# A macaron transformer kernel: x's first slice ahead of the first weights, and the norm's turn two slices later

## What is computed

```python
def rms_norm(x, g):
    y = xf * lax.rsqrt(jnp.mean(xf * xf, axis=-1, keepdims=True) + EPS)
    return (y * g).astype(x.dtype)

def swiglu(x, w_gate, w_up, w_down):        # 1024 -> 2816 -> 1024
    return (jax.nn.silu(x @ w_gate) * (x @ w_up)) @ w_down

for i in range(2):
    x = x + 0.5 * swiglu(rms_norm(x, ffn1_norm[i]), ...)
    x = x + (even_mixer, odd_mixer)[i](rms_norm(x, mix_norm[i]), ...)
    x = x + 0.5 * swiglu(rms_norm(x, ffn2_norm[i]), ...)
```

## Time and profile before

| what | value |
|---|---|
| median of three runs | 1895.54 us (1895.01 to 1895.95) |
| the profiled execution's time | 1896.99 us |
| its span, first to last instruction | 1895.2 us |
| TensorE busy | 1865.2 us, 98% |
| DVE busy | 1458.9 us, 77% |
| ACT busy | 1022.7 us, 54% |
| POOL busy | 193.8 us, 10% |

### The profile page before, as it was taken

One profiled execution on the slowest core, in us unless ns is written; L12 is line 12 of the kernel. 1 busy time (PEld: TensorE's weight loads), 2 busy tenths in 40 slices (PEclk: granted clock), 3 DMA queues, 4 the chain that ended last, 5 costly groups with the idle time before them and its releaser, 6 DMA issues.

```text
span 1895.2 us, 31481 instructions
## 1 busy us (share of the span) xinstructions
PE 1865.2 (98%) x11916; PEld 1661.6 (88%) x11916; DVE 1458.9 (77%) x2346; ACT 1022.7 (54%) x1656; POOL 193.8 (10%) x251
## 2 busy tenths in 40 slices
PE   7999999999999999999999999999999999999999
PEld 6899899888779899998889989887778789899997
DVE  8879587577679788597877859657988879697684
ACT  7546264477776355364645526455456766364451
POOL 1311010000001011010011101011111001011010
PEclk9999999999999999999999999999999999999999
DMA  7666662221136565463465556176765376575441
GB/s 235 162 201 184 177 165 66 100 67 68 57 111 178 173 167 152 149 174 109 134 175 156 151 150 173 45 174 159 166 152 132 79 203 170 163 185 158 133 117 67
DMA packets 94790, 271.67 MB, mean 143 GB/s; under 512 B 10504, under 2 KB 10760, under 8 KB 94640
## 3 DMA queue, kind: packets, MB, share of 16 engines
q1 hardware_dynamic: 63456, 201.22, 31.0%
q0 software_dynamic: 29232, 64.50, 19.9%
q10 hardware_dynamic: 1952, 3.93, 1.1%
HBM read 223.07 MB, written 2.77 MB: 119 GB/s over the span
## 4 chain that ended last, share of the span: by engine, by line
PE 88%; DVE 7%; ACT 3%; issue 2%; DMA 0%; ACTq 0%; DVEq 0%
PE ps_unit L817 13%; PE ps_unit L818 13%; PE ps_unit L819 13%; PE ps_y L880 6%; PE ps_y L882 6%; PE ps_y L881 6%; PE ps_s L880 4%; PE ps_s L882 4%; PE ps_s L881 4%; PE ps_t L880 4%; PE ps_t L882 4%; PE ps_t L881 4%; PE ps_s L817 1%; PE ps_s L818 1%; PE ps_s L819 1%
## 5 line engine op out<-in xcount | busy, mean ns | idle before, releaser
L1429 ACT ACTIVATE gw_hi<-gu 128x512 fp32r<-128x512 f32 (+1 forms) x400 | 318.9, 799 | 153.5 <-PE ps_s L882 69.0
L1961 DVE TENSOR_TENSOR gw_lo<-gu,gw_hi 128x512 fp32r<-128x512 f32 (+1 forms) x400 | 354.4, 901 | 40.5 <-ACT gw_hi L1429 33.5
L817 PE MATMUL ps_unit<-a_hi,w_hi 128*128 128x512 f32 x892 | 351.7, 394 | 5.5 <-DVE w_lo L1891 2.8
L818 PE MATMUL ps_unit<-a_lo,w_hi 128*128 128x512 f32 x892 | 348.3, 390 | 0.0
L819 PE MATMUL ps_unit<-a_hi,w_lo 128*128 128x512 f32 x845 | 329.4, 390 | 0.0
L1363 ACT ACTIVATE w_hi<-raw 128x1024 fp32r<-128x1024 f32 (+1 forms) x125 | 125.3, 1003 | 304.6 <-PE ps_unit L819 300.7
L817 PEld LDWEIGHTS ps_unit<-a_hi,w_hi 128*128 128x128 f32 x892 | 167.8, 188 | 45.2 <-DVE w_lo L1891 5.1
L2098 DVE TENSOR_TENSOR t<-ps_unit,half 128x512 f32<-128x512 f32 x96 | 66.4, 691 | 171.8 <-PE ps_unit L819 171.4
L818 PEld LDWEIGHTS ps_unit<-a_lo,w_hi 128*128 128x128 f32 x892 | 167.9, 188 | 33.0
L819 PEld LDWEIGHTS ps_unit<-a_hi,w_lo 128*128 128x128 f32 x845 | 158.9, 188 | 33.7
L1891 DVE TENSOR_TENSOR w_lo<-raw,w_hi 128x1024 fp32r<-128x1024 f32 (+1 forms) x125 | 143.8, 1151 | 13.0 <-ACT w_hi L1363 12.9
(11 more groups left out here) (332 smaller groups left out, 4875.4 us busy)
## 6 DMA issues: line engine op xcount, KB each, us to landing
gu<-gu_stream_dram SPq DMA_DIRECT2D x176, 512.0 KB, 5.2
raw<-w_stream_dram SPq DMA_DIRECT2D x136, 512.0 KB, 3.3
gu<-gu_stream_dram SPq DMA_DIRECT2D x80, 256.0 KB, 3.0
gu<-gu_stream_dram POOLq DMA_DIRECT2D x80, 256.0 KB, 4.1
gu<-gu POOLq DMA_DIRECT2D x80, 256.0 KB, 3.3
w_lo<-raw POOLq DMA_DIRECT2D x28, 512.0 KB, 5.3
raw<-w_stream_dram SPq DMA_DIRECT2D x32, 384.0 KB, 3.9
w_lo_3rd<-raw POOLq DMA_DIRECT2D x15, 512.0 KB, 5.1
```

The lines of the kernel that those rows point to most:

```text
L817: pe.matmul(ps, lhs_hi, rhs_hi, start=first, stop=False)
L818: pe.matmul(ps, lhs_hi, rhs_lo, start=False, stop=False)
L1429: act.activation(gw_hi[:, w, :], src, ACT.Copy).then_inc(gw_hi_done, 1)
L1961: dve.tensor_tensor(gw_lo[:, w, :], src, gw_hi[:, w, :].bitcast(F32), ALU.subtract).then_inc(gw_lo_done, 1)
```

## The change

Two edits. In the second plain tile `spread_norm` moves from behind slice 4 (the third in order) to behind slice 1 (the fifth). This holds in all four feed-forward phases. At the start of the kernel, slice 0 of x is loaded first on SP instead of on ACT's queue, its high and low parts are made before the first weights' parts, and its square and the copy into `acc` come after both parts of the first weights instead of between them.

```diff
+            x_load(0)
             gu_load(0)
             for d in range(1, KT):
                 x_load(d)
...
                     if k == 0:
                         square_sum(i)
-                    if k == 4:
+                    if k == 1:
                         spread_norm(i)
...
             def split_x(i, d):
-
+                high_x(i, d)
+                square_x(i, d, d)
+
+            def high_x(i, d):
                 negative = PHASES[i] == "ffn" and d % 2
                 scale = minus(i * KT + d) if negative else gain("norm", i * KT + d)
                 act.activation(xs_hi[:, d, :], xt_tile(d), ACT.Copy, scale=scale).then_inc(x_hi_done, 1)
-                square_x(i, d, d)
...
             act.dma_start(vec[:, :], vec_in).then_inc(vec_landed, 16)
-            act.dma_start(xt_tile(0), xt_in[0]).then_inc(x_landed[0], 16)
...
             act.wait_ge(vec_landed, 16)
+            act.wait_ge(x_landed[0], 16)
+            high_x(0, 0)
             act.wait_ge(s1_loaded[0], 16)
             for part in range(2):
                 act.activation(gw_hi[:, part, :], gu[:, part, :], ACT.Copy).then_inc(gw_hi_done, 1)
-                if part == 0:
-                    act.wait_ge(x_landed[0], 16)
-                    split_x(0, 0)
+            square_x(0, 0, 0)
             plain_high(0, 1)
...
             def split_x(i, d):
+                low_x(i, d)
+                square_added(i, d)
...
             dve.wait_ge(vec_landed, 16)
+            low_x(0, 0)
             for part in range(2):
                 dve.wait_ge(gw_hi_done, part + 1)
                 dve.tensor_tensor(gw_lo[:, part, :], gu[:, part, :], gw_hi[:, part, :].bitcast(F32), ALU.subtract).then_inc(gw_lo_done, 1)
-                if part == 0:
-                    split_x(0, 0)
+            square_added(0, 0)
             plain_low(0, 1)
```

More of the change, by code:

```diff
@@ L1893, in split_x, with low_x @@
             def split_x(i, d):
+                low_x(i, d)
+                square_added(i, d)
+            def low_x(i, d):
                 negative = PHASES[i] == "ffn" and d % 2
@@ L1898, in split_x @@
                                          ALU.mult, ALU.subtract).then_inc(x_lo_done, 1)
-                square_added(i, d)
             def square_added(i, p):
```

## The result

The changed kernel takes 1900.38 us in the median of nine runs, against 1895.59 us for the kernel before: ratio 1.0025, 95% interval 1.0016 to 1.0033. It is slower by 4.8 us, and the forecast was 1900.3. The profiled execution took 1903.53 us, the longest of the nine, so its rows are compared with rows and not with the medians.

A forecast was written before the change was run, and what follows sets the result against it. PE, busy 98% of the span, was taken as the bound; − 1.4 us at the start plus 4 × 1.56 for the transposes gave + 4.8, so 1895.54 + 4.8 = 1900.3 us, range 1897.0 to 1902.6.

The forecast's parts named there:

- What bounds: Whole kernel: PE is busy 98% of the span, so an edit counts only by what it changes in PE's idle time.
- The gain at the start: Kernel start: second weights' high part at 7.11 us instead of 8.53, so PE's unbroken work starts 1.42 us sooner.
- `vec`'s release at 4.93: Kernel start: ACT's wait for `vec` ends at 4.93 us as before and decides when slice 0's high part begins.
- hidden by 0.2 us: Kernel start: second weights land by 6.9 us, before ACT needs them at 7.11, so their landing costs nothing.
- The clock rise: PE at the start: rise follows 5.9 us of unbroken work, keeping 1.4 us; other cases keep 0.7 or 2.9.
- The landings: DMA at the start: the skill's fit gives 3.2 us for 512 KB, trace 3.9 and 5.3; by it some 2 us gain.
- The move of the transposes: Second plain tile, four ffn phases: DVE copies 2.54 us later, slack 1.14, bubble 0.11; PE pays 1.56 us per phase.
- Slack larger than read: Rival, chain behind DVE's copy: delay is absorbed, only the start's gain counts, 1894.1 us; chance 0.08.
- Given back later: Rival, down projection's first group ends: PE's 0.6 us waits absorb the delay, 2.4 us in all, 1897.9; chance 0.12.
- PE pays the whole: Rival, ffn phases: a step without slack makes PE pay DVE's whole delay, + 10.6 us, 1904.7; chance 0.10.
- The start gains nothing: Rival, kernel start: second weights land 1.4 us later than worked out, `plain_high` waits, 1901.8 us; chance 0.04.
- The first phase: First ffn phase: DVE, arriving at 30.2 us, waits for the transposes until 32.0; same price, 1.56 us.

The follow-up runs named there:

- e1_start_only: Changed kernel with the transposes back behind slice 4, so only the start edit against the kernel before: 1894.17 us against 1895.88, ratio 0.9991.
- e7_squares_later: Start edit alone, with slice 0's square and copy into `acc` moved still later, against the kernel before: 1894.93 us, ratio 0.9995.
- e10_load_only: Kernel before with only slice 0 of x loaded first on SP, ACT's and DVE's order unchanged: 1894.87 us against 1895.81, ratio 0.9995.
- e2_turn_only: Kernel before with only the transposes moved behind slice 1, start unchanged: 1901.63 us against 1895.88, ratio 1.003.
- e6_filled: Changed kernel with work not needing `rstd` moved ahead of the wait on DVE and ACT, against the kernel before: 1894.88 us against 1895.85, ratio 0.9993.
- e3_turn_after_6: Changed kernel with the transposes behind slice 6, the fourth in order, against the kernel before: 1894.6 us, ratio 0.9992.
- e4_turn_after_3: Changed kernel with the transposes behind slice 3, the sixth in order, against the kernel before: 1907.57 us, ratio 1.0057.
- e8_turn_after_5: Changed kernel with the transposes behind slice 5, the seventh in order, against the kernel before: 1915.2 us against 1895.81, ratio 1.0103.

## Why the prediction was right

- **What bounds.** PE's chain with one order of other engines beside it: right. The moved transposes cost at PE what exceeded the slack, to 0.1 us in each of the four phases.
- **The gain at the start**, 1.4 us: measured − 1.7 alone, 1.31 at PE's second start. The size was right, the steps to it were not all, and that it came out is partly luck. I kept `vec`'s release at 4.93 from the kernel before; with the new load it landed by 4.1 in every profile. So the first weights decide, and not `vec`. They released ACT at 5.65 in the kernel after, at the 5.6 that I had named as the point past which I would be wrong, and the two errors nearly cancelled (7.22 against 7.11 for the second weights). In the other profiles they landed where I had them, by 5.2. There PE's second start was 1.7 to 1.9 us sooner where the second weights came in time, and 0.9 to 1.0 where they did not (e1_start_only, e7_squares_later, e10_load_only): that these are hidden by 0.2 us did not hold there.
- **The clock rise.** It came after some 5 us of work instead of 5.9, and PE gains half of that difference, 0.5 us; inside the bounds given. So PE was 1.8 us ahead behind the rise, and not 1.4. No row stood behind the 2.9 us by which the rise might come sooner; the earliest here, 3.0 us after the second start in e7_squares_later, is just that. The Trainium skill (TensorE: Matmul & The Clock Gate, Part 1) says that the default state is throttled and that activity releases it. The profiles agree, but loosely: the two with the old start rose at 16.4 and 17.5 us, the ten with the new one or its load between 13.4 and 15.9, and from the start of unbroken work it took between 3.0 and 6.2. So up to 1.6 us, half of that spread, is chance in any one execution, and the forecast's 1.4 can be right for the median only.
- **The landings.** The fit of the Trainium skill (DMA: Bandwidth & Descriptors, Anatomy of one DMA) gives, as an estimate, 2.6 us for 256 KB; slice 0 landed in 3.1. So the trace is slower than the fit here too. The section states the fit for transfers that the gpsimd path issues, and these are issued on SP's queue, so it was a rough guide to begin with, which the prediction did not say. By the fit the gain would have been some 2 us; 1.7 was measured alone, too near to tell the two apart.
- **The move of the transposes**, 1.56 us a phase, 6.2 in all: 1.47 to 1.57 in each phase of the trace, 6.1 in all, and + 5.75 in the times of e2_turn_only; the 0.45 between is under what the times can tell. PE's wait came in two pieces, for the low weights and for the second of the four `ps_s` steps. The sum had left the first out as falling inside the second, and that held in the total. That a wait in the queue and not the position costs is shown by e6_filled, the slack of 1.1 us by e3_turn_after_6 (DVE 1.04 us late, at most 0.2 us at PE).
- **The rivals.** "Slack larger than read" is excluded by e2_turn_only, + 3.4 us at least, and by e3_turn_after_6 and e4_turn_after_3 on both sides of the edge. "Given back later" is excluded: the waits at the ends of groups stay as they were, five, 2.8 us in all, before and after. "PE pays the whole" is excluded by the 0.5 and 0.4 us waits and the 1.57 us that they cost. "The start gains nothing" is excluded by PE's second start, 0.9 to 1.9 us sooner in every profile with the new load.
- **The first phase** cost nearly as the others, 1.47 us: two PE waits of 0.53 and 0.45 us. DVE waited 1.3 us, under the 1.8 expected; 0.3 of that is what PE had gained beyond the 1.4.

No version is faster than the kernel before beyond doubt. The fastest, e1_start_only, is 1.7 us under it with an interval that touches 1.0.

## What to carry to other kernels

Moving a step to where its own engine does not wait is not free when another engine takes the result in order: price the delay along the consumer's queue, subtract the slack at the row where the bounding engine first needs its end, and pay only the rest. If the step must be late, put work ahead of the wait that does not need it. Read the slack from the tightest consumer, and check every phase that shares the code, not the one for which the edit was made.

## What was not expected

A wait of 1.9 us on TensorE can halve the granted clock for some 3 us, at 0.9 us of cost between the same matmuls of one kernel (0.7 each in the times: 1.4 us over the queue's price, two of four phases). It did so in four of eight such waits in two profiles of the same kernel, in different phases. Waits of 3.3 us did it in four of four, at 0.9 us each in the times. In the second mixer the clock fell in all twelve profiles: in eleven behind or during a wait of 1.3 us, and in e8_turn_after_5, at 1495.9 us, with no wait over 0.2 us in the 20 us ahead. So a short wait alone does not say whether the clock will fall; what else has to come together no run here separates.

At the start the granted-clock column does not show the half rate. Stretches of the kernel after (the same columns as above, granted clock third from the end):

```profile
11.00:15.00 4.00, 4.00 (x11) 3.12 (x10) 4.00 (x7) 3.98 (x8) 0.00 (x0) 1.00 1.03 384
16.00:20.00 4.00, 4.00 (x19) 3.23 (x18) 4.00 (x7) 2.99 (x6) 0.08 (x1) 1.00 1.04 406
```

It reads 1.00 in both, while the matmuls of 512 columns stand 0.43 us apart in the first and 0.23 in the second. There the pitch has to be read, not the column.
